# An encoder layer on one core: two heads' value products in turns, last rows picked with plain 0/1 matrices in fp32r halves, one turn moved

## The chip, the core and the metric

The kernel runs on 1 core of one Trainium2 chip. The metric is the device time of one execution in microseconds, the median of the runs. Engines: TensorE (PE in the profile; PEld is its weight load), VectorE (DVE), ScalarE (ACT), GpSimd (POOL), SyncE (SP, which here only issues DMAs).

## What is computed

One layer of a streaming encoder over 544 tokens (512 of a new stream, 32 of a running one) of width 1024, all in float32:

```python
h = rmsnorm(x, g_norm_mix)
cq, ckv, kpe, gq, gk, gv, glr, gr, ga, gb = split_cols(h @ w_in)
o_a = mla_attention(...)          # 8 heads, 64-wide values, chunk-causal
o_g, s_new = gla(...)             # 4 heads, matrix state 128 x 256, decaying
o_b = rmsnorm(o_g, g_gla_norm) * silu(gr)
merged = sigmoid(ga) * (o_a @ w_branch_a) + sigmoid(gb) * (o_b @ w_branch_b)
x = x + merged @ w_out
y = hier_moe(rmsnorm(x, g_norm_ffn), ...)   # 32 experts, the best 2 of one group of 8 per token
x = rmsnorm(x + y, g_norm_final)
```

An expert is `(silu(xb @ w_gate) * (xb @ w_up)) @ w_down` with 1024 x 512 weights: 6 MB per expert, 32 experts. A token's two expert rows are added with two gates.

## The kernel before

**Products in three parts.** The large projections run as fp32r matmuls. A weight tile `raw` is split in a high half `whi` (ScalarE, `high`) and a low half `wlo` (GpSimd, `split`, L909), the activations likewise, and `product` (L1055) adds high x high, high x low and low x high: 48 matmuls of 272 columns for eight blocks of K. The order of products is a list written out by hand (`weight_tiles`, `outputs`). Results go to two PSUM slots `proj` in turn; the next product but one waits until ScalarE or VectorE has read its slot (`proj_read`).

**Attention.** 40 units `u` = (head pair, row block, head of the pair). Row blocks 0 to 3 have 128 queries and 1 to 4 blocks of keys, block 4 (the running stream) has 32 queries and three blocks. The loop L1216 is a software pipeline on TensorE: `scores(u)`, a third of a filling projection (`product_part`, 16 matmuls, until the list is used up), `turn_probs(u - 2)` (transposes into bank 2), `pv(u - 3)` (value product into bank 3, head `a` in partitions 64a to 64a + 63). VectorE takes the maximum and normalises, ScalarE exponentiates (`exps`) and copies the turned probabilities out (`copy_turned`, which may not overwrite `probT[u % 2]` before the value product of unit u - 2). `copy_out` on VectorE splits the pair's output after both heads. All of these are fp32 matmuls, each of which is two records in the trace.

**GLA and branches.** After the recurrent part, VectorE normalises outputs (`normed_output`, L2368; L2383 for the running stream), ScalarE copies the high half (`o_high`, 0 to 4), and the low half `ob_lo` is made by GpSimd for the first `EARLY_LOW` parts (`low_output`, L917, placed in GpSimd's queue behind the split of `wa` 5 and ahead of that of `gb` 0) and by VectorE for the rest (L2390). TensorE meanwhile runs `ga` 5 and `wa` 5, then `gb` 0 and `wb` 0. `gb` 0 needs the slot of `ga` 5, read by the sigmoid of `gate_value(0, "ga", 5)` (L1907), and its own split weights; `wb` 0 needs the slot of `wa` 5, read by VectorE's `branch(0, 5)`, and all five parts of `ob_lo`.

**Routing.** VectorE finds each token's experts, slots and gates. `on_lanes` (L1498) multiplies one-hot matrices (`lanes`, slot of the block; values by block of 64 slots) to give each lane its token: twenty fp32 records each, two halves of 64 lanes in turns. `unread` and the loop L1491 are idle products. Two times five transposes (L1528) then spread the gates of the tokens for experts 30 and 31 along the free dimension. GpSimd gathers the token rows by these numbers; `turn_rows` (L1564) turns them.

**Experts.** Weights flow in three sets of buffers (`load_expert`, L817) as sets come free. Per expert `up` (L1538, L1540: two halves of the array in turns), Silu on ScalarE, the product on VectorE (L2541), `turn_hidden` (L1547), `down` (L1554, L1555). Rows of experts 0 to 29 are scattered to DRAM and read back (`zc`, L890) once all are stored. The load of `zc` stands in the queue behind the weights.

**The end.** Experts 30 and 31 skip the way through DRAM. Their rows stay in `yo`, and `last_rows` (L1631) multiplies `pick[s]`, a matrix of slot by token holding the gate where they meet, with `yo` in two row halves of 64 slots, into PSUM; for row blocks 1 to 3 `second_rows` (L1642) adds the gated second rows. VectorE adds the first rows with their gates (`add_gated`, L2617), then PSUM (`add_last`, L2624), ScalarE sums the squares (L1717) and takes the root (L1719), VectorE applies `final` (L2635). Expert 30's turn stands between the up products of 30 and 31.

## Time and profile before

| | us |
|---|---|
| median of 3 runs (lowest to highest) | 1121.83 (1120.65 to 1122.44) |
| the profiled execution | 1119.33 |
| its span, first to last instruction | 1117.5 |
| TensorE busy | 1028.3 (92%) |
| VectorE, ScalarE, GpSimd busy | 384.0, 282.0, 221.3 |
| attention's value products (first to last start) | 105.5 to 250.3 |
| first products of the `gb`, `wb` branch | 421.4 |
| expert weights: first request | 562.5 |
| first down rows of expert 30 turned | 1077.1 |
| mean DMA rate over the span | 239 GB/s |

A matmul's busy time is modelled to its end, so records that follow each other overlap: the distance between two starts tells what a group costs the engine, and where groups are merged in a timeline row, the start of the next row ends it. In brackets stands the idle time ahead of a row and what ended it. An arrow points from what is read to what is written.

### The profile page before, as it was taken

The numbers are of one execution on the slowest core, as the hardware profiler recorded it, in microseconds if no ns is written. First come the engines' busy times: TensorE is split into PE (matmuls) and PEld (weight loads), VectorE is DVE, ScalarE is ACT, GpSimd is POOL, SyncE is SP. The second block draws the span as 40 slices with busy tenths as digits, with TensorE's granted clock in tenths as the row PEclk, the third lists the DMA queues.
The fourth block names the chain that finished last, engine by engine and source line by source line (L and its number), as shares of the span: only waits on it lengthen the run. The fifth ranks groups of instructions, "written<-read, shape, count | busy, mean of one in ns | idle before, by whom it ended". The sixth has DMA issues, their size and how long they took to land.

```text
span 1117.5 us, 15305 instructions
## 1 busy us (share of the span) xinstructions
PE 1028.3 (92%) x6339; PEld 701.7 (63%) x6339; DVE 384.0 (34%) x729; ACT 282.0 (25%) x455; POOL 221.3 (20%) x127
## 2 busy tenths in 40 slices
PE   8999999999999999999999899988888888778886
PEld 6996777869998879999998333333333333333232
DVE  7246232233587492421344322111111111111017
ACT  5435434346456542222213100000000000000003
POOL 0331122112322363434330011100111110110000
PEclk9999999999999989999999999988888998988898
DMA  8343411212212113253285999999999999999994
GB/s 224 89 91 88 159 39 40 56 38 76 58 48 56 50 57 94 78 165 103 78 352 225 345 427 428 425 427 425 427 427 427 427 428 428 426 429 426 426 412 156
DMA packets 108943, 267.57 MB, mean 239 GB/s; under 512 B 21821, under 2 KB 88797, under 8 KB 95666
## 3 DMA queue, kind: packets, MB, share of 16 engines
q1 hardware_dynamic: 104178, 258.06, 60.1%
q0 software_dynamic: 4704, 8.64, 2.0%
q8 instruction: 46, 0.75, 0.3%
q14 instruction: 15, 0.12, 0.0%
HBM read 256.12 MB, written 18.17 MB: 245 GB/s over the span
## 4 chain that ended last, share of the span: by engine, by line
PE 39%; DMA 23%; DVE 4%; issue 2%; ACT 2%; SPq 0%; DVEq 0%; ACTq 0%
DMA we<-in_w_exp_up 23%; PE proj L1055 17%; PE proj L1538 12%; PE proj L1554 3%; PE bank L1380 1%; PE bank L1430 1%; DVE xsT L2549 1%; PE proj L1336 1%; PE bank L1564 1%; ACT ex L1878 0%; PE proj L1540 0%; PE bank L1031 0%; PE bank L1631 0%; PE bank L1517 0%; SPq L817 0%
## 5 line engine op out<-in xcount | busy, mean ns | idle before, releaser
L1538 PE MATMUL proj<-we,xsT 128*64 128x512 f32 x512 | 255.7, 658 | 61.4 <-DMA we<-in_w_exp_up 51.8
L1540 PE MATMUL proj<-we,xsT 128*64 128x512 f32 x512 | 256.1, 658 | 0.0
L909 POOL TENSOR_TENSOR wlo<-raw,whi 128x1024 fp32r<-128x1024 f32 x68 | 155.8, 2292 | 396.7 <-PE proj L1055 369.1
L1538 PEld LDWEIGHTS proj<-we,xsT 128*64 128x64 f32 x512 | 74.3, 151 | 210.1 <-issue 197.1
L1055 PE MATMUL proj<-hT_hi,whi 128*128 128x272 f32 x688 | 146.6, 295 | 3.8 <-ACT sg L1907 3.8
L1055 PE MATMUL proj<-hT_hi,wlo 128*128 128x272 f32 x688 | 144.6, 292 | 0.0
L1055 PE MATMUL proj<-hT_lo,whi 128*128 128x272 f32 x688 | 144.5, 292 | 0.0
L2541 DVE TENSOR_TENSOR hg<-hg,proj 64x512 f32<-64x512 f32 x32 | 22.1, 690 | 308.8 <-ACT hg L2050 294.0
L2050 ACT ACTIVATE hg<-proj 64x512 f32<-64x512 f32 x30 | 17.8, 592 | 422.0 <-PE proj L1540 422.0
L1554 PE MATMUL proj<-we,hT 128*64 128x512 f32 x256 | 115.2, 592 | 1.1 <-DVE hT L2544 1.1
L1555 PE MATMUL proj<-we,hT 128*64 128x512 f32 x256 | 115.2, 592 | 0.0
L1055 PEld LDWEIGHTS proj<-hT_hi,whi 128*128 128x128 f32 x688 | 109.1, 190 | 6.6 <-ACT sg L1907 4.0
L1055 PEld LDWEIGHTS proj<-hT_lo,whi 128*128 128x128 f32 x688 | 109.0, 191 | 1.6 <-issue 0.9
L1055 PEld LDWEIGHTS proj<-hT_hi,wlo 128*128 128x128 f32 x688 | 108.6, 191 | 1.6 <-issue 0.9
L947 POOL DMA_INDIRECT expert_out<-yo,sidx x30 | 29.9, 997 | 386.7 <-DVE sidx L2561 386.7
L1696 ACT CAST whi<-raw 128x1024 fp32r<-128x1024 f32 x70 | 69.6, 997 | 109.7 <-PE proj L1055 102.1
L1554 PEld LDWEIGHTS proj<-we,hT 128*64 128x64 f32 x256 | 34.9, 137 | 71.3 <-issue 69.3
L1540 PEld LDWEIGHTS proj<-we,xsT 128*64 128x64 f32 x512 | 74.2, 151 | 0.0
L2558 DVE COPY yo<-proj 128x512 f32<-128x512 f32 x30 | 20.8, 692 | 66.1 <-PE proj L1555 66.1
L2211 DVE TENSOR_REDUCE stat<-bank 128x1 f32<-128x128 f32 (+4 forms) x40 | 19.2, 482 | 58.9 <-PE bank L1182 50.3
L1555 PEld LDWEIGHTS proj<-we,hT 128*64 128x64 f32 x256 | 34.9, 137 | 0.0
L1794 ACT ACTIVATE prob<-bank,stat 128x128 f32<-128x128 f32 (+4 forms) x40 | 20.9, 522 | 42.5 <-DVE stat L2211 42.2
(366 smaller groups left out, 1436.6 us busy)
## 6 DMA issues: line engine op xcount, KB each, us to landing
we<-in_w_exp_gate SPq DMA_DIRECT2D x31, 2048.0 KB, 32.2
we<-in_w_exp_up SPq DMA_DIRECT2D x31, 2048.0 KB, 36.8
we<-in_w_exp_down SPq DMA_DIRECT2D x31, 2048.0 KB, 38.8
raw<-in_w_in SPq DMA_DIRECT2D x43, 512.0 KB, 3.8
x_rows<-in_x_prompt SPq DMA_DIRECT2D x8, 512.0 KB, 4.8
raw<-in_w_branch_b SPq DMA_DIRECT2D x8, 512.0 KB, 4.1
raw<-in_w_out SPq DMA_DIRECT2D x8, 512.0 KB, 3.8
zc<-expert_out SPq DMA_DIRECT2D x4, 1024.0 KB, 17.3
```

The lines of the kernel that those rows point to most:

```text
L909: nc.gpsimd.tensor_tensor(lo[:, 0:c], raw[n % NRAW][:, 0:c], hi[:, 0:c].bitcast(F32), ALU.subtract).then_inc(w_split, 1)
L947: pool.indirect_dma_start(out=ys[:, :], out_offset=bass.IndirectOffsetOnAxis(ap=sidx[s][:, 0:1], axis=0), in_=yo[:, s, :], in_offset=None, ...
L1055: mm = pe.matmul(proj[:, slot, half, 0:HALF], w[:, at:at + P], r[:, k, half * HALF:(half + 1) * HALF], start=(m == 0), stop=(m == len(term ...
L1538: pe.matmul(proj[0:SLOTS, s, 0, :], xsT[:, k, cols], wg[:, k * FF:(k + 1) * FF], start=(k == 0), stop=(k == KD - 1))
L1540: mm = pe.matmul(proj[64:64 + SLOTS, s, 0, :], xsT[:, k, cols], wu[:, k * FF:(k + 1) * FF], start=(k == 0), stop=(k == KD - 1))
L1554: pe.matmul(proj[0:SLOTS, s, 1, :], hT2[:, s, k, :], wd[:, k * D:k * D + FF], start=(k == 0), stop=(k == 3))
L1555: mm = pe.matmul(proj[64:64 + SLOTS, s, 1, :], hT2[:, s, k, :], wd[:, k * D + FF:(k + 1) * D], start=(k == 0), stop=(k == 3))
L1696: nc.scalar.copy(whi[n % NHIGH][:, 0:c], raw[n % NRAW][:, 0:c]).then_inc(w_high, 1)
L1794: nc.scalar.activation(prob[u % 3][0:r, 0:n], bank[0:r, u % 2, 0:n], ACT.Exp, bias=stat[0:r, 1, u:u + 1], scale=-1.0, accum_out=stat[0:r, ...
L2211: v.tensor_reduce(stat[0:r, 1, u:u + 1], bank[0:r, u % 2, 0:n], AX.X, ALU.min).then_inc(negmax_ready, 1)
L2541: v.tensor_tensor(hg[0:SLOTS, s, :], hg[0:SLOTS, s, :], proj[64:64 + SLOTS, s, 0, :], ALU.mult).then_inc(done, 1)
L2558: v.tensor_copy(yo[:, s, :], proj[:, s, 1, :])
```

## The change

1. `pv` takes a pair of heads: for each block of keys the matmul of head 0 and that of head 1 follow each other. It is issued at u = 2v + 4, where so far the second head's stood; the first head's stood one step earlier.
2. `EARLY_LOW` is 2 instead of 3: part 2 of `ob_lo` goes from GpSimd to VectorE. On ScalarE `gate_value(0, "ga", 5)` comes before `o_high(3)` and `o_high(4)`.
3. The gates of experts 30 and 31 are brought to the lanes by two `on_lanes` products (2 columns) instead of ten transposes. They scale the rows of `yo`, and `pick[s]` is a plain 0/1 matrix. `yo` is held in fp32r as a high half (ScalarE) and a low half (VectorE, `low_rows`), and each pick has two fp32r matmuls for one in fp32; the pick for row block 0 waits for the low half.
4. The turn of expert 30's hidden rows moves from between the up products of 30 and 31 to the middle of those of 31.
5. ScalarE runs a one-column Sqrt behind the last Silu, and waits for `picks_ready` before the last rows.
6. A few buffers move: `xsb2` (used only if some expert has more than 64 rows) to behind `g_fin`, `yo_lo` to its place, and everything from the weight ring on by 64 bytes.

```diff
--- before.py
+++ after.py
@@ -121,7 +121,7 @@
-EARLY_LOW = 3
+EARLY_LOW = 2
@@ -340,7 +340,8 @@
     sidx = [R(f"sidx{n}", [P, 1], U32) for n in range(2)]
     gate = R("gate", [P, 2, NT])
-    last_gates = R("last_gates", [P, NT, 2])
+    last_gates = R("last_gates", [P, 2, NT, 2])
+    last_slots = R("last_slots", [P, 2])
     RING = R.at
...
@@ -527,6 +531,7 @@
     down_done = sem("down_done")
     yo_ready = sem("yo_ready")
+    low_y = sem("low_y")
     ys_zeroed = sem("ys_zeroed")
...
@@ -693,9 +697,12 @@
     U_ = Region(RT)
-    pick = [U_(f"pick{s}", [P, TOK]) for s in range(2)]
-    xsb2 = U_("xsb2", [P, D])
+    pick = [U_(f"pick{s}", [P, TOK], F32R) for s in range(2)]
+    yo_lo = U_("yo_lo", [P, 2, FF], F32R)
     assert U_.at <= LAST
+    xsb2 = nc.alloc_sbuf_tensor_at("xsb2", [P, D], F32, offset=G_FIN + D * 4)
+    assert G_FIN + 2 * D * 4 <= W_G2 + GH * DK * 4
     numbers = con("rope")
@@ -1195,24 +1202,26 @@
             mm.then_inc(probT_done, 1)
-        def pv(u):
-            hp, i, a = UNITS[u]
-            h = 2 * hp + a
+        def pv(v):
+            hp, i, _ = UNITS[2 * v]
             r = unit_shape(i)[0]
-            v = u // 2
-            pe.wait_ge(probT_copied, u + 1)
-            if a == 0 and v >= 1:
+            pe.wait_ge(probT_copied, 2 * v + 2)
+            if v >= 1:
                 pe.wait_ge(oa_done, v)
             blocks = key_blocks(i)
             for b, kr_, vb in blocks:
-                mm = pe.matmul(bank[64 * a:64 * a + 64, 3, 0:r],
-                               V[0:kr_, vb, h * VD:(h + 1) * VD], probT[u % 2][0:kr_, b * r:(b + 1) * r],
-                               start=(b == 0), stop=(b == len(blocks) - 1))
-            mm.then_inc(pv_done, 1)
+                for a in range(2):
+                    h = 2 * hp + a
+                    mm = pe.matmul(bank[64 * a:64 * a + 64, 3, 0:r],
+                                   V[0:kr_, vb, h * VD:(h + 1) * VD], probT[a][0:kr_, b * r:(b + 1) * r],
+                                   start=(b == 0), stop=(b == len(blocks) - 1))
+            mm.then_inc(pv_done, 2)
         keys(0)
         keys(1)
         NU = len(UNITS)
+        assert NU % 2 == 0 and all(a == u % 2 for u, (_, _, a) in enumerate(UNITS))
         for u in range(NU + 3):
@@ -1226,8 +1235,8 @@
             if 2 <= u < NU + 2:
                 turn_probs(u - 2)
-            if u >= 3:
-                pv(u - 3)
+            if u >= 4 and u % 2 == 0:
+                pv(u // 2 - 2)
@@ -1521,12 +1530,8 @@
         pe.wait_ge(last_gates_ready, 1)
-        for s in range(2):
-            row = proj[:, s, :, :].rearrange("p a b -> p (a b)")
-            for i in range(NT):
-                r = ROWS[i]
-                mm = pe.transpose(row[:, i * P:i * P + r], last_gates[0:r, i, s:s + 1].to_broadcast([r, P]), ident[0:r, 0:r])
-            mm.then_inc(gate_rows_done, 1)
+        on_lanes(proj[:, 0, 0, 0:2], 0, last_gates, True, False)
+        on_lanes(proj[:, 0, 0, 0:2], 1, last_gates, False, True).then_inc(gate_rows_done, 1)
@@ -1628,7 +1633,12 @@
             for half in range(2):
                 rows_ = slice(64 * half, 64 * half + 64)
-                mm = pe.matmul(out[0:r, half, :], pick[s][rows_, i * P:i * P + r], yo[rows_, s, :], start=start, stop=stop)
+                pe.matmul(out[0:r, half, :], pick[s][rows_, i * P:i * P + r], yo_hi[rows_, s, :], start=start, stop=False)
+            if i == 0:
+                pe.wait_ge(low_y, s + 1)
+            for half in range(2):
+                rows_ = slice(64 * half, 64 * half + 64)
+                mm = pe.matmul(out[0:r, half, :], pick[s][rows_, i * P:i * P + r], yo_lo[rows_, s, :], start=False, stop=stop)
             if stop:
@@ -1641,7 +1651,11 @@
                 pe.matmul(out[:, half, :], second[:, i - 1, :], zc[i][:, 1, half * FF:(half + 1) * FF], start=start, stop=False)
         def up_half(k):
+            if k:
+                pe.wait_ge(act_done[0], PAIRS)
+                turn_hidden(0, hT2_done)
             for part in range(2):
@@ -1657,8 +1671,6 @@
             pe.wait_ge(n0[part], loads)
         up(0, slice(0, SLOTS), w0[0], w0[1], up_done)
-        pe.wait_ge(act_done[0], PAIRS)
-        turn_hidden(0, hT2_done)
         up(1, slice(SLOTS, P), w1[0], w1[1], up_done, up_half)
@@ -1983,9 +1995,9 @@
         nc.scalar.activation(ors_d[:, :, :], bank[:, 1, 0:GH * DEC].rearrange("p (h l) -> p h l", l=DEC), ACT.Sqrt, bias=eps_col[:, :])\
             .then_inc(o_rms, 1)
+        gate_value(0, "ga", 5)
         o_high(3)
         o_high(GH)
-        gate_value(0, "ga", 5)
         out_of("wa", 5)
@@ -2065,13 +2077,16 @@
         act.wait_ge(up_done, NE)
         nc.scalar.activation(hg[0:SLOTS, 1, :], proj[0:SLOTS, 1, 0, :], ACT.Silu).then_inc(silu_done, 1)
+        nc.scalar.activation(st_x[:, 1, 0:1], eps_col[:, :], ACT.Sqrt)
         act.wait_ge(all_stored, 1)
+        act.wait_ge(picks_ready, 1)
         act.wait_ge(down_done, NE - 1)
-        nc.scalar.copy(yo[:, 0, :], proj[:, 0, 1, :]).then_inc(last_y, 1)
+        nc.scalar.mul(yo_hi[:, 0, :], proj[:, 0, 1, :], last_slots[:, 0:1]).then_inc(last_y, 1)
         act.wait_ge(hT2_done, NE)
         nc.scalar.copy(hT2[:, 1, :, :], bank[:, 3, 0:4 * SLOTS].rearrange("p (k l) -> p k l", k=4)).then_inc(hT2_copied[1], 1)
         act.wait_ge(down_done, NE)
-        nc.scalar.copy(yo[:, 1, :], proj[:, 1, 1, :]).then_inc(last_y, 1)
+        nc.scalar.mul(yo_hi[:, 1, :], proj[:, 1, 1, :], last_slots[:, 1:2]).then_inc(last_y, 1)
@@ -2516,8 +2531,8 @@
         run(v.reciprocal(gate[:, 0, :], r5[2]))
         run(v.tensor_tensor(gate[:, 1, :], gate[:, 0, :], rd, ALU.mult))
-        run(v.tensor_tensor(both_gates, O[:, :, :, NE - 2:NE], gate[:, :, :].unsqueeze(3).to_broadcast([P, 2, NT, 2]), ALU.mult))
-        v.tensor_tensor(last_gates[:, :, :], both_gates[:, 0], both_gates[:, 1], ALU.add).then_inc(last_gates_ready, 1)
+        v.tensor_tensor(last_gates[:, :, :, :], is_blk[:, :, :, NE - 2:NE], gate[:, :, :].unsqueeze(3).to_broadcast([P, 2, NT, 2]), ALU.mult)\
+            .then_inc(last_gates_ready, 1)
@@ -2530,10 +2545,10 @@
         dve.wait_ge(meta_ready, 1)
         dve.wait_ge(late_loaded, 32)
+        dve.wait_ge(gate_rows_done, 1)
+        v.tensor_copy(last_slots[:, :], proj[:, 0, 0, 0:2])
         for s in range(2):
-            dve.wait_ge(gate_rows_done, s + 1)
-            row_ = proj[:, s, :, :].rearrange("p a b -> p (a b)")[:, 0:TOK]
-            last = v.scalar_tensor_tensor(pick[s][:, :], numbers, G1[:, NE - 2 + s:NE - 1 + s], row_, ALU.is_equal, ALU.mult)
+            last = v.tensor_scalar(pick[s][:, :], numbers, G1[:, NE - 2 + s:NE - 1 + s], None, ALU.is_equal)
         last.then_inc(picks_ready, 1)
@@ -2611,6 +2626,11 @@
             gated(s, act_done[s])
+        def low_rows(s):
+            dve.wait_ge(last_y, s + 1)
+            v.scalar_tensor_tensor(yo_lo[:, s, :], proj[:, s, 1, :], last_slots[:, s:s + 1], yo_hi[:, s, :].bitcast(F32),
+                                   ALU.mult, ALU.subtract).then_inc(low_y, 1)
         def add_gated(i, c):
@@ -2635,9 +2655,11 @@
                 .then_inc(y_last, 1)
+        low_rows(0)
         add_gated(0, 0)
         step.settle()
         add_gated(0, 1)
+        low_rows(1)
         add_gated(1, 0)
```

## Rows read from the trace of the kernel before

**Rows 1.** the page's 40 slices: share of the DMA engines, in tenths

```profile
DMA  8343411212212113253285999999999999999994
```

**Rows 2.** busy time of each engine by stretch, with granted clock and DMA

```profile
core 0: us, PE busy (x) PEld busy (x) DVE busy (x) ACT busy (x) POOL busy (x), PEclk, DMA share, GB/s
200.00:220.00 20.00, 20.00 (x139) 16.18 (x137) 6.18 (x21) 8.00 (x20) 4.73 (x2) 1.00 0.12 29
...
422.30:425.60 3.30, 3.30 (x17) 3.30 (x17) 0.00 (x0) 0.91 (x1) 2.37 (x1) 0.51 0.00 0
426.00:430.00 4.00, 4.00 (x34) 4.00 (x33) 0.00 (x0) 0.77 (x2) 0.66 (x1) 1.00 0.46 131
633.00:1068.00 435.00, 372.85 (x1650) 145.41 (x1648) 76.02 (x176) 17.75 (x30) 43.55 (x43) 0.91 1.01 426
1102.40:1115.10 12.70, 5.71 (x22) 1.42 (x18) 12.26 (x14) 4.33 (x9) 0.00 (x0) 0.87 0.34 136
```

**Rows 3.** timeline, TensorE, attention: start, duration, line, out<-in, shapes, count

```profile
105.53 0.43 PE L1208 MATMUL bank<-probT,V 128*64 128x128 f32 x2
105.90 0.91 PE L1178 MATMUL bank<-kcat,qT 96*128 96x384 f32 x2
...
212.17 1.09 PE L1208 MATMUL bank<-probT,V 128*64 128x128 f32 x8
213.19 0.49 PE L1178 MATMUL bank<-kcat,qT 96*128 96x128 f32 x2
...
220.28 0.64 PE L1208 MATMUL bank<-probT,V 128*64 128x32 f32 x6
```

**Rows 4.** timeline of TensorE where tiles of 32 and 64 columns take turns

```profile
343.14 1.08 PE L1283 MATMUL bank<-ex 128*32 128x128 f32 x32
344.15 0.66 PE L1287 MATMUL bank<-cst,ex 128*128 128x128 f32 x4
...
616.73 0.92 PE L1498 MATMUL bank<-token_at,lanes 128*64 128x48 f32 x20 [0.25 <-DVE token_at L2493]
617.58 0.92 PE L1498 MATMUL bank<-is_blk,lanes 128*64 128x48 f32 x20
```

**Rows 5.** timeline of TensorE at the end of attention

```profile
249.31 1.19 PE L1208 MATMUL bank<-probT,V 128*64 128x32 f32 x12 [0.54 <-DVE oa_lo L2230]
```

**Rows 6.** timeline of all engines around the first branch products

```profile
401.50 1.42 DVE L2368 SCALAR_TENSOR_TENSOR gqk<-gqk,gains,ors 128x512 f32<-128x512 f32 x2
...
408.20 7.54 POOL L917 TENSOR_TENSOR ob_lo<-gqk,ob_hi 128x1024 fp32r<-128x1024 f32 x3
...
410.84 0.37 ACT L1984 ACTIVATE ors_d<-bank,eps_col 128x128 f32<-128x128 f32 x1
411.08 5.22 DVE L2368 SCALAR_TENSOR_TENSOR gqk<-gqk,gains,ors 128x512 f32<-128x512 f32 x2
...
415.71 2.83 POOL L909 TENSOR_TENSOR wlo<-raw,whi 128x1024 fp32r<-128x1024 f32 x1
...
419.41 1.28 ACT L1907 ACT_TABLE_LOAD   x1
...
421.38 0.52 PE L1055 MATMUL proj<-hT_hi,whi 128*128 128x272 f32 x2 [3.76 <-ACT sg L1907]
```

**Rows 7.** timeline of TensorE in the routing stage

```profile
620.25 1.52 PE L1528 MATMUL proj<-cst,last_gates 128*128 128x128 f32 x10
```

**Rows 8.** timeline of TensorE and VectorE behind the last weights

```profile
1077.12 0.69 PE L1547 MATMUL bank<-cst,hg 64*128 64x64 f32 x4 [1.41 <-DVE hg L2541]
...
1091.89 3.83 DVE L2617 SCALAR_TENSOR_TENSOR x_rows<-zc,gate,x_rows 128x1024 f32<-128x1024 f32 x3 [5.69 <-DMA zc<-expert_out]
...
1094.62 1.02 PE L1631 MATMUL bank<-yo,pick 64*128 64x512 f32 x4
...
1098.66 1.22 DVE L2624 TENSOR_TENSOR x_rows<-x_rows,proj 128x1024 f32<-128x1024 f32 x1 [0.32 <-PE proj L1631]
...
1102.49 1.22 DVE L2624 TENSOR_TENSOR x_rows<-x_rows,bank 128x1024 f32<-128x1024 f32 x1 [1.34 <-PE bank L1631]
```

More of the change, by code:

```diff
@@ L465, in _build @@
     hT2 = K_("hT2", [P, 2, 4, SLOTS])
+    YO = K_.at
     yo = K_("yo", [P, 2, FF])
+    yo_hi = nc.alloc_sbuf_tensor_at("yo_hi", [P, 2, FF], F32R, offset=YO)
     W_ = Region(K_.at)
@@ L685, in _build @@
     expert = T_("expert", [P, 2, NT])
-    both_gates = T_("both_gates", [P, 2, NT, 2])[:, :, :, :]
     extra = T_("extra", [P, NE])[:, :]
```

## The prediction

> **What bounds the kernel now.** I read the page's 40 slices first, for the regime of each part, then busy time by stage, and then the timeline engine by engine where the edits lie. Over the last 17 slices the DMA engines are full [rows 1]; from 633 to 1068 us they carry 426 GB/s with a share of 1.01, while TensorE is idle for 62 of 435 us [rows 2]. This is the stream of 32 experts' weights. A faster matmul inside it buys nothing: its length is bytes over rate. It starts when the branch products are done, so all that ends earlier ahead of it moves the whole stream, and the end with it. Ahead of it TensorE is the bound: in attention it is busy 20.00 of 20.00 us at clock 1.00 [rows 2]. Two stretches therefore matter: TensorE's path before the stream, and what follows the stream's last bytes.
>
> **Value products in turns.** Now each unit (one head, one row block) has its own value product in the left or right 64 columns of the array. It occupies TensorE for 105.90 − 105.53 = 0.37 us with one block of keys and 213.19 − 212.17 = 1.02 us with four [rows 3], so (1.02 − 0.37)/3 = 0.217 us per further block: 0.37, 0.58, 0.80, 1.02. The sample's block, with 32 columns moved, takes 0.58 (six records, of which the last drains beyond it; bounds 0.52 and 0.64 [rows 3]). One head: 3.35 us; eight: 26.8 us, all on the path.
> The change issues both heads' matmuls block by block in turns. What would two half-array matmuls side by side cost? The trace has such orders elsewhere. 32 records in 32-column tiles of the same 128 moved columns take 344.15 − 343.14 = 1.01 us, that is 0.126 us for four side by side [rows 4]. 20 records in 64-column tiles, alternating halves and moving 48 columns, take 617.58 − 616.73 = 0.85 us, 0.085 per pair [rows 4]. A single record now has 0.217/2 = 0.108. So a pair costs between 0.108 (nothing lost) and 0.126; I take 0.117, the middle, as nothing says which end. Over 4 head pairs × 20 records that is 0.7 us lost against perfect overlap. Pairing saves 13.4 − 0.7 = 12.7 us.
> "TensorE: Matmul & The Clock Gate" of the Trainium skill (section on LDWEIGHTS) speaks against the small block: a load costs its columns divided by 1.2, 53 ns for 64, so 107 ns for two heads' loads. By that rule six pairs of the sample block would cost 0.64 us and the four pairs together save 0.2 to 0.3 us less. The rows disagree: two 64-column loads and their matmuls fit in 85 ns [rows 4].
> What is late next: the copy of an even unit's turned probabilities must now wait for the value products of the pair before it, as these are issued one unit later. ScalarE queues behind that wait the next exponential and an eviction. TensorE wants the copy only after the next scores and 16 filling matmuls (about 2 us), and the copy follows the pair at once, so I charge nothing there. At the end of attention no filling is left. There the chain is value pair, copy of unit 38, turn of unit 39, copy, last pair, and the 0.54 us that TensorE already waits for VectorE [rows 5] stays. Adding the copies and turns as they follow each other, I charge 0.9 us, with bounds 0.3 and 1.6. **Attention: −11.8 us, bounds −10.5 and −13.**
>
> **Order on ScalarE and EARLY_LOW 2.** TensorE stands still for 3.76 us until 421.38, on the sigmoid of `ga` 5 [rows 6]. ScalarE is free from 411.2, but makes two copies `o_high` first, which wait for VectorE. It turns to the sigmoid only at 419.41 (table load 1.28, then 0.62) [rows 6]. Put ahead of them, it needs just the product of `ga` 5, which ends 24 matmuls of 4.0/34 = 0.118 us [rows 2] before the standstill at 417.6, so at about 414.8; the sigmoid is out by 415.4 to 416.7. The next bar is the weight split of `gb` 0 on GpSimd, ending at 415.71 + 2.83 = 418.5 behind three `low_output` (7.54 us) [rows 6]. With two of them (5.03) GpSimd is free at 413.2, starts after the product at 414.8, and ends by 417.6 at the latest. Neither is later than 417.6: the standstill goes.
> Third bar: the `wb` 0 product, 48 matmuls (5.7 us) later at 423.3, needs all parts of `ob_lo` and VectorE's `branch(0, 5)`. VectorE's two `L2368` last 5.22 us beside GpSimd's work against 1.42 without it [rows 6]; with one GpSimd operation less they end some 1.5 us earlier. VectorE gains the moved subtraction: bounds 1.2 us (half of GpSimd's 2.51) and 1.2 + 2.4 if it is held again. I add up to VectorE done at 422.3, or 424 when held at each step; I take no wait, bound 0.7.
> Here the rule bears against the edit: "GPSIMD Engine Reference" of the Trainium skill (Specifications) says that GpSimd's SBUF interfaces are shared with VectorE, with contention for operations with two SBUF inputs. A subtraction moved to VectorE is such an operation. The 5.22 against 1.42 us agree.
> After the standstill the granted clock is 0.51 for 3.3 us: 17 records, where 34 take 4.0 at full clock [rows 2]. Its loss, 3.3 − 17 × 4.0/34 = 1.3 us, goes with the standstill. **Branch stage: −3.8 − 1.3 = −5.1, bounds −3 and −5.4.**
>
> **Gates on lanes.** Ten transposes (1.52 us with the drain, 1.35 of pitch) [rows 7] become two `on_lanes` of 0.85 each [rows 4]: +0.35 us ahead of the first turn of gathered rows. Weights already requested keep the DMA engines busy meanwhile, so part is hidden: **+0.2, bounds 0 and +0.4.** The picks on VectorE become cheaper but were hidden behind the gather. One small operation goes; nobody waits for it.
>
> **Behind the stream.** The turn of expert 30's hidden rows (0.69 us after 1.41 of waiting) [rows 8] moves inside the next up products. But VectorE's tail starts when the stored rows land at 1091.89 [rows 8], behind the weights in the queue. The turn buys slack and no time: 0. Picks: two fp32 records per half become two fp32r ones. Four side by side take 0.9 to 1.0 us now [rows 8]; by the products' pace (0.118 us for 272 columns) the high and low records of 512 columns take 2 × 0.22 = 0.44. TensorE gains 0.45 at each of ten picks. VectorE pays two low halves; the second (0.7 us, PSUM and SBUF into 512 columns) lies on its path. VectorE waited 0.32 us for picks before 1098.66 and 1.34 before 1102.49 [rows 8]; from then on it is busy 12.26 of 12.70 us [rows 2, 8]. So the end comes earlier by 1.34 + 0.32 − 0.7 = 1.0 us at most, by −0.3 if a wait is left. The load of the Sqrt table (a table load takes 1.28 us [rows 6]) goes under the last products; in the tail it lies beside VectorE's combinations, which are busy without a wait for it, and is worth 0. **Tail: −1.0, bounds −1.3 and +0.7.**
>
> **Sum.** −11.8 − 5.1 + 0.2 − 1.0 = −17.7 us. The profiled execution took 1119.3 us (span 1117.5), so it would be 1101.6. The median of the runs shown, 1121.8, lies 2.5 above the profiled one, so I forecast 1104.1.
>
> **Rivals.**
> A. Two heads' products do not run side by side, their records being short and fp32 in two passes. Then 12.7 comes back: 1116.8. Against it stand both groups of rows 4, for it only that neither has exactly this form. 0.07.
> B. The branch stage keeps a wait in a new place: VectorE, held by GpSimd as in the 5.22 us, delivers `ob_lo` and `branch(0, 5)` 2 us or more after 423.3, and the slow clock follows again (1.3). That gives 1107.4 to 1109. 0.10.
> C. Row halves in fp32r don't overlap: a pick costs 4 × 0.22 = 0.88, as now, and the low halves come on top: tail +0.7, 1105.8. 0.10, within the main range.
> D. Slower than before: attention falls to the half clock. The pace of rows 2 makes each us of full-clock work 1.65 us; the gain of 17.7 is gone once 27 us of attention's work run so, and at 35 us the time is 1127. Against it: clock 1.00 with TensorE full, and the odd units lose matmuls but no filling. 0.03.
> The forecast has 0.70.
>
> **Range and chances.** The parts' bounds, taken together with one unit of run spread (1120.65 to 1122.44), give 1100 to 1108 for the forecast alone. B reaches to 1109, so 1099.5 to 1109.5 leaves out A, D and about 0.06 of larger surprises. A measurement of this kernel tells about 0.2% (2.2 us) from no change. Faster by more: 0.96; within: 0.01; slower: 0.03.
>
> **What would show it.** In the changed profile: value products of a four-block pair within 1.0 to 1.15 us, none in odd units, attention over 11 to 12 us earlier; no standstill before `gb` 0 and no slow clock behind it; first expert weights requested some 17 us earlier; 426 GB/s as before; VectorE without idle time between the first combination and the last row. It is wrong if value records follow one another at 0.108 us, if the standstill has moved to `wb` 0, or if the stream's length changes.

## The result, and the profile after

The changed kernel takes 1102.76 us (median of 4 executions, 1101.24 to 1103.72) beside 1121.24 us for the kernel before: 18.5 us less, ratio 0.9833 with a 95% interval of 0.9816 to 0.9851. The forecast was 17.7 us less. The profiled execution took 1103.72 us (span 1101.6), that of before 1119.33. In a second comparison the same kernel gained only 15.4 us (below, x9); what differs between the two turned out to be the main lesson. One of the nine executions of the kernel before in the last series below took 2498.14 us; it counts in the median given there, but not in the intervals.

| us, profiled executions | before | after | difference |
|---|---|---|---|
| first scores of attention | 96.08 | 97.01 | +0.93 |
| from there to the first gate product behind attention | 154.93 | 142.27 | −12.66 |
| from there to the last 512-column means | 143.11 | 143.06 | −0.05 |
| last 512-column means to the first of the small means | 12.53 | 12.52 | −0.01 |
| from there to `wb` 0 (the branch stage) | 22.38 | 16.82 | −5.56 |
| `wb` 0 to the first expert's up product | 196.90 | 197.35 | +0.45 |
| first up product to the first stored rows added | 465.96 | 467.99 | +2.03 |
| from there to the end of the last `final` (the tail) | 23.18 | 22.19 | −0.99 |

Attention of after, timeline of TensorE (start, duration, line, out<-in, shapes, count, and in brackets the idle time ahead and what ended it). It answers to [rows 3] and [rows 5]:

```profile
206.45 1.09 PE L1216 MATMUL bank<-probT,V 128*64 128x128 f32 x16
207.47 0.49 PE L1185 MATMUL bank<-kcat,qT 96*128 96x128 f32 x2
...
235.57 0.31 PE L1202 MATMUL bank<-cst,prob 32*128 32x32 f32 x3 [0.85 <-DVE prob L2234]
235.81 1.09 PE L1216 MATMUL bank<-probT,V 128*64 128x128 f32 x16
237.43 0.31 PE L1202 MATMUL bank<-cst,prob 32*128 32x32 f32 x3 [0.53 <-ACT probT L1819]
238.10 0.66 PE L1216 MATMUL bank<-probT,V 128*64 128x32 f32 x12 [0.37 <-ACT probT L1819]
239.28 1.38 PE L1247 MATMUL bank<-w_g,glr 96*128 96x512 f32 x4 [0.52 <-DVE oa_lo L2245]
```

Sixteen records of two heads take 207.47 − 206.45 = 1.02 us. In [rows 3] eight records of one head took exactly that. The last rows show what came in place of the filling work: waits at the end of attention.

The branch stage of after, timeline of ScalarE, GpSimd and VectorE, and one stretch of busy time with granted clock. They answer to [rows 6] and to the half-clock row in [rows 2]:

```profile
402.86 0.63 ACT L1919 ACTIVATE sg<-proj 128x544 f32<-128x544 f32 x1 [2.30 <-PE proj L1062]
```

```profile
396.41 4.76 POOL L924 TENSOR_TENSOR ob_lo<-gqk,ob_hi 128x1024 fp32r<-128x1024 f32 x2
402.97 2.41 POOL L916 TENSOR_TENSOR wlo<-raw,whi 128x1024 fp32r<-128x1024 f32 x1 [1.81 <-PE proj L1062]
```

```profile
399.29 3.09 DVE L2383 SCALAR_TENSOR_TENSOR gqk<-gqk,gains,ors 128x512 f32<-128x512 f32 x2
...
405.72 4.89 DVE L2405 TENSOR_TENSOR ob_lo<-gqk,ob_hi 128x1024 fp32r<-128x1024 f32 x3
410.53 0.71 DVE L2352 TENSOR_TENSOR msum<-proj,sg 128x544 f32<-128x544 f32 x1
```

```profile
core 0: us, PE busy (x) PEld busy (x) DVE busy (x) ACT busy (x) POOL busy (x), PEclk, DMA share, GB/s
404.00:411.70 7.70, 7.70 (x64) 7.70 (x63) 7.25 (x6) 2.73 (x4) 4.60 (x2) 1.00 0.41 111
```

TensorE is busy in every microsecond up to `wb` 0, at clock 1.00. GpSimd's split for `gb` 0 ends at 402.97 + 2.41 = 405.38, and `gb` 0 starts at 405.67: 0.29 us are left there. VectorE's `branch(0, 5)` ends at 411.24, and `wb` 0 starts at 411.68: 0.44 us are left before the third bar bites.

The tail of after, timeline of VectorE, against [rows 8]:

```profile
1077.02 2.61 DVE L2637 SCALAR_TENSOR_TENSOR x_rows<-zc,gate,x_rows 128x1024 f32<-128x1024 f32 x2 [2.62 <-DMA zc<-expert_out]
1079.55 0.74 DVE L2631 SCALAR_TENSOR_TENSOR yo_lo<-proj,last_slots,yo_hi 128x512 fp32r<-128x512 f32 x1
...
1084.11 1.22 DVE L2644 TENSOR_TENSOR x_rows<-x_rows,proj 128x1024 f32<-128x1024 f32 x1
...
1086.63 1.22 DVE L2644 TENSOR_TENSOR x_rows<-x_rows,bank 128x1024 f32<-128x1024 f32 x1
```

The two waits for picks (0.32 and 1.34 us) are gone and the low half (0.74) has come: 23.18 − 22.19 = 0.99 us saved.

Two rows of the table have no term in the prediction. Attention's first scores start between 96.08 us (before) and 99.26 us (x2) in the 14 profiles of this document, in kernels whose code ahead of them is the same, so the 0.93 us say nothing of the change. And the second expert ran partly at the half clock in this execution; from its first up product to its first down product it takes 8.61 us, against 6.92 before, which is 1.69 of the 2.03 us:

```profile
core 0: us, PE busy (x), PEclk, DMA share, GB/s
616.00:623.00 7.00, 5.50 (x22) 0.76 1.00 383
```

Whether the change has a part in that is open: it is seen in three of the nine profiles whose kernels have the new gates and picks (after, x4, x11), and in none of the five without.

### The profile page after: what moved, and what is told of

Same layout as the page of the kernel before. It is cut to its first block, busy times and chain, and to the rows that moved or that the text cites. A ratio compares the mean times of both kernels' runs of the same rounds, so it can differ in the third digit from the quotient of the medians.

```text
span 1101.6 us, 15368 instructions
## 1 busy us (share of the span) xinstructions
PE 1004.5 (91%) x6369; PEld 696.1 (63%) x6369; DVE 390.0 (35%) x732; ACT 281.0 (26%) x456; POOL 218.9 (20%) x126
## 4 chain that ended last, share of the span: by engine, by line
PE 38%; DMA 26%; DVE 4%; issue 2%; ACT 1%; SPq 0%; DVEq 0%; POOLq 0%; ACTq 0%
DMA we<-in_w_exp_up 24%; PE proj L1062 18%; PE proj L1543 11%; PE proj L1559 3%; DMA zc<-expert_out 1%; PE bank L1389 1%; PE bank L1439 1%; DMA expert_out<-yo,sidx 1%; PE bank L1569 1%; PE proj L1345 1%; DVE x_rows L2637 1%; DVE xsT L2564 1%; ACT ex L1890 1%; PE proj L1545 0%; DVE x_rows L2644 0%
## 5 line engine op out<-in xcount | busy, mean ns | idle before, releaser
L1543 PE MATMUL proj<-we,xsT 128*64 128x512 f32 x512 | 249.1, 644 | 69.6 <-DMA we<-in_w_exp_up 61.5
L1545 PE MATMUL proj<-we,xsT 128*64 128x512 f32 x512 | 249.5, 644 | 0.0
L2062 ACT ACTIVATE hg<-proj 64x512 f32<-64x512 f32 x30 | 17.7, 590 | 424.0 <-PE proj L1545 424.0
L1185 PE MATMUL bank<-kcat,qT 96*128 96x128 f32 (+4 forms) x80 | 30.0, 456 | 0.4 <-ACT kcat L1793 0.4
```

The costliest lines, as they stand in the source:

```text
L1185: mm = pe.matmul(bank[0:r, u % 2, 0:n], qT[0:QK, h, q0:q0 + r], kcat[hp % 2][0:QK, a, k0:k0 + n], start=True, stop=(i == 4))
L1543: pe.matmul(proj[0:SLOTS, s, 0, :], xsT[:, k, cols], wg[:, k * FF:(k + 1) * FF], start=(k == 0), stop=(k == KD - 1))
L1545: mm = pe.matmul(proj[64:64 + SLOTS, s, 0, :], xsT[:, k, cols], wu[:, k * FF:(k + 1) * FF], start=(k == 0), stop=(k == KD - 1))
```

## The experiments

Three series of executions of the kernel before stand beside them: 1119.45 us for x1 to x4, 1120.03 us for x5 to x7 and x9, 1120.89 us for x8 and x10 to x12. All differences from here on are against these. x5 to x7 and x9 ran on another chip than the other experiments. What is read from a trace comes from one execution of each kernel. Rows of busy time without a head line have the columns of the second expert's row above (stretch, its length, TensorE's busy time with its records, granted clock, DMA share, GB/s).

### Does each part carry its own term? (x1, x2, x3)

x1_pairs_only puts only the paired value products into the kernel before:

```diff
...
-            if u >= 3:
-                pv(u - 3)
+            if u >= 4 and u % 2 == 0:
+                pv(u // 2 - 2)
```

> The kernel before with the paired value products alone. Theory (two heads' products run side by side at the price of one): attention 12.7 us shorter, so 1121.2 - 12.7 = 1108.5 us, a four-block pair in 1.02 us, and the standstill before the gb branch still there. Rival 1 (most of the gain is the later, single place of the pair, with fewer interruptions, and not the overlap): the time is the same here too, so this kernel does not tell it apart; x4_pair_in_sequence does. Rival 2 (the gain of attention is partly given back in the branch stage, where VectorE and GpSimd were hidden by it): over 1110 us.

Measured: 1108.72 us, 10.7 less (ratio 0.99, 0.9883 to 0.9917). In its trace attention takes 142.35 us, 12.58 less than before, and the standstill ahead of `gb` 0 is still there with 3.73 us. Attention's term is confirmed in the trace; the time shows 2 us less of it. Most of that is given back in the tail, which is 24.93 us long here, 1.75 more than before. VectorE's rows of x1, to be read against [rows 8]:

```profile
1080.18 2.61 DVE L2617 SCALAR_TENSOR_TENSOR x_rows<-zc,gate,x_rows 128x1024 f32<-128x1024 f32 x2 [3.96 <-DMA zc<-expert_out]
...
1085.72 1.22 DVE L2624 TENSOR_TENSOR x_rows<-x_rows,bank 128x1024 f32<-128x1024 f32 x1 [1.49 <-PE bank L1631]
...
1088.70 1.22 DVE L2624 TENSOR_TENSOR x_rows<-x_rows,proj 128x1024 f32<-128x1024 f32 x1 [0.56 <-PE proj L1631]
...
1092.53 1.22 DVE L2624 TENSOR_TENSOR x_rows<-x_rows,bank 128x1024 f32<-128x1024 f32 x1 [1.34 <-PE bank L1631]
```

It now waits three times for picks. The stored rows landed at 1080.18, but the first pick behind the last expert's products starts only at 1083.69, 3.51 us later (before, 1091.89 and 1093.65: 1.76 us). From that pick to the end it is 21.42 us in both. So in these two kernels the end hangs on TensorE's last products and not on the stored rows. Why those products came later here is open.

x2_branch_only:

```diff
-EARLY_LOW = 3
+EARLY_LOW = 2
...
+        gate_value(0, "ga", 5)
         o_high(3)
         o_high(GH)
-        gate_value(0, "ga", 5)
```

> The kernel before with ScalarE's gate of ga 5 ahead of the two high copies and with EARLY_LOW 2, nothing else. Theory: standstill of 3.8 us and the slow clock behind it (1.3 to 1.7 us) both go, 1121.2 - 5.5 = 1115.7 us, wb 0 starts without a wait. Rival (the wait moves to wb 0, on VectorE's branch(0, 5) or its low parts): about 2 us less gain, 1117.5 to 1119 us.

Measured: 1114.52 us, 4.9 less (0.9961, 0.9943 to 0.9979). No idle time ahead of `gb` 0 or `wb` 0; from the small means to `wb` 0 it takes 16.82 us against 22.38, as in the changed kernel.

x3_rest_only leaves out both and keeps gates, picks, turn and Sqrt:

```diff
+            if k:
+                pe.wait_ge(act_done[0], PAIRS)
+                turn_hidden(0, hT2_done)
...
-        for s in range(2):
-            row = proj[:, s, :, :].rearrange("p a b -> p (a b)")
...
+        on_lanes(proj[:, 0, 0, 0:2], 0, last_gates, True, False)
+        on_lanes(proj[:, 0, 0, 0:2], 1, last_gates, False, True).then_inc(gate_rows_done, 1)
```

> The kernel before with only the parts behind the branch stage: gates on lanes, plain picks in two halves, the moved turn, the early Sqrt. Theory: tail -1.0, routing +0.2, so 1121.2 - 0.8 = 1120.4 us, hardly to be told from no change in the time; in the trace the stretch from VectorE's first combination of stored rows to the last final operation is 22.2 us against 23.2. Rival (the low halves on VectorE's path cost what the picks save): 23.2 us or more, 1121.4 us or more.

Measured: 1119.6 us, no difference that can be told (0.9999, 0.9988 to 1.001; 1115.41 to 1121.62 in ten executions). In the trace the tail is 1088.99 to 1111.18, 22.19 us, against 23.18: the 1.0 us is there. But the trace also shows where it is spent: from `wb` 0 to the first expert's up product it takes 197.93 us against 196.90, 1.03 us more. In the five profiles without the new gates and picks that distance is 196.88 to 196.94 us, in the nine with them 197.35 to 198.52.

### Overlap, or only one place? (x4)

```diff
-            for b, kr_, vb in blocks:
-                for a in range(2):
+            for a in range(2):
+                for b, kr_, vb in blocks:
```

> The changed kernel with the matmuls of a pair in another order: all blocks of one head, then all of the other, at the same place in the queue, same work. Theory (the gain is the overlap of the two halves of the array while they take turns): a four-block pair takes 2.04 us instead of 1.02 and the kernel 1102.8 + 13.4 = 1116.2 us. Rival (the gain comes from issuing the pair at one place): within 2 us of 1102.8.

Measured: 1107.7 us, 11.75 less than before (0.9902, 0.9884 to 0.992). Both expectations missed: the order costs about 5 us (1107.7 against 1102.76, and 5.36 in the trace of attention), not 13.4 and not nothing. Its timeline of TensorE:

```profile
110.41 0.44 PE L1216 MATMUL bank<-probT,V 128*64 128x128 f32 x4
110.78 0.91 PE L1185 MATMUL bank<-kcat,qT 96*128 96x384 f32 x2
...
117.75 0.66 PE L1216 MATMUL bank<-probT,V 128*64 128x128 f32 x8
118.34 1.13 PE L1185 MATMUL bank<-kcat,qT 96*128 96x512 f32 x2
...
134.34 1.58 PE L1216 MATMUL bank<-probT,V 128*64 128x128 f32 x16
135.85 0.49 PE L1185 MATMUL bank<-kcat,qT 96*128 96x128 f32 x2
...
142.00 1.22 PE L1216 MATMUL bank<-probT,V 128*64 128x32 f32 x12
143.15 0.70 PE L1185 MATMUL bank<-kcat,qT 96*128 96x256 f32 x2
```

| us from one start to the next | two heads apart (before, twice the single of [rows 3]) | in sequence (x4) | in turns (after) |
|---|---|---|---|
| 1 block | 0.74 | 0.37 | 0.37 |
| 2 blocks | 1.16 | 0.59 | 0.59 |
| 3 blocks | 1.60 | 1.07 | 0.81 |
| 4 blocks | 2.04 | 1.51 | 1.02 |
| sample, 32 columns moved | 1.16 | 1.15 | 0.59 |
| sum | 6.70 | 4.69 | 3.38 |

Over four head pairs, standing next to each other saves 4 × 2.01 = 8.0 us and taking turns another 4 × 1.31 = 5.2; the stage of x4 is 147.63 − 142.27 = 5.36 us longer than that of the changed kernel. So two heads in sequence overlap too, but only in part. With 128 columns moved, up to four records of the second head run beside the last of the first. A single record takes 0.108 us, and 0.15 us of each distance belong to no record (0.37 − 2 × 0.108). By that 8 + 8 records take (1.51 − 0.15)/0.108 = 12.6 steps, 6 + 6 take 8.5, 4 + 4 take 4. With 32 columns nothing overlaps in sequence (1.15 = 2 × 0.58). Why, stays open.

### Which bar holds the branch stage? (x5, x6)

x5_order_only has the order of x2 with EARLY_LOW 3; x6_low_only has EARLY_LOW 2 with the old order.

> The kernel before with ScalarE's order alone changed; EARLY_LOW stays 3. Theory (two bars stand one behind the other): the sigmoid is no longer late, but GpSimd's split for gb 0 is, behind three low parts: it ends near 418.5 in the times of before, 0.9 us behind the last product of wa 5. The standstill shrinks from 3.8 to 0.9 to 1.3 us, so 2.5 to 2.9 us are gained, 4.2 if the slow clock behind it goes too; 1115 to 1117 us. Rival (ScalarE's order is all that counts): the standstill is gone and the gain is 5.5 us, as with both edits.

Measured: 1117.4 us, 2.6 less (0.9977, 0.9967 to 0.9988). Timeline of TensorE and GpSimd of x5, and busy time behind the standstill:

```profile
419.06 0.49 PE L1055 MATMUL proj<-hT_hi,whi 128*128 128x272 f32 x2 [1.82 <-POOL wlo L909]
```

```profile
408.55 7.59 POOL L917 TENSOR_TENSOR ob_lo<-gqk,ob_hi 128x1024 fp32r<-128x1024 f32 x3
416.10 5.19 POOL L909 TENSOR_TENSOR wlo<-raw,whi 128x1024 fp32r<-128x1024 f32 x2
```

```profile
419.06:423.50 4.44, 4.44 (x23) 0.62 0.62 168
```

The releaser has changed from ScalarE's `sg` to GpSimd's `wlo`, as the second bar demands, but 1.82 us remain, not 0.9 to 1.3, and the half clock stays.

> The kernel before with EARLY_LOW 2 alone; ScalarE keeps its order. Theory: the sigmoid still stands behind the two copies, but VectorE is held by GpSimd for a shorter time, so that its parts come about 1.3 us earlier and the standstill is 2.5 us instead of 3.8; 1.3 us gained, 1118 us. Rival (the low part on GpSimd is what delays the product): gain of 3.8 us or more.

Measured: 1118.23 us, 1.8 less (0.9983, 0.9973 to 0.9993). The standstill is 2.37 us and still ends with the sigmoid. So each edit alone leaves a wait on the other's bar, and only both together remove it. The profile of x6 has a second wait, though, one of 1.99 us ahead of `ga` 5 (below), which the profile of before lacks. Its 2.37 us are therefore not simply 3.76 less what the edit saves.

### Does the moved turn buy anything? (x7)

```diff
-            if k:
-                pe.wait_ge(act_done[0], PAIRS)
-                turn_hidden(0, hT2_done)
...
+        pe.wait_ge(act_done[0], PAIRS)
+        turn_hidden(0, hT2_done)
         up(1, slice(SLOTS, P), w1[0], w1[1], up_done, up_half)
```

> The changed kernel with expert 30's turn back between the up products of experts 30 and 31. Theory (the turn buys slack, no time): the same time as the changed kernel on this chip within 0.5 us, and VectorE's tail begins when the stored rows land, in both. Rival (the turn brings expert 30's rows early enough to matter): 0.7 us or more slower, with VectorE waiting in the tail.

Measured: 1102.59 us (1099.84 to 1106.45), not to be told from x9. In the trace VectorE's tail begins with the stored rows in both, but here it waits 0.26 us for expert 31's high half at `low_rows(1)`, and the tail is 22.53 us against 22.22 in x9. That is not shown to be the turn's work: x8, x10 and x12 below have the moved turn, and the same wait (0.20 to 0.22 us) and the same tail (22.47 to 22.50 us). VectorE's row of x10:

```profile
1078.07 0.75 DVE L2634 SCALAR_TENSOR_TENSOR yo_lo<-proj,last_slots,yo_hi 128x512 fp32r<-128x512 f32 x1 [0.22 <-ACT yo_hi L2092]
```

In these four profiles the stored rows landed 465.5 to 465.7 us behind the first up product, in the others of kernels with the new picks 466.1 us or more. From the first up product to the end x7 takes 488.19 us and the other three 487.97 to 488.13. The turn buys no time that can be told.

### The changed kernel once more (x9)

> The changed kernel as it is, on the chip of these comparisons and in more rounds. If the parts measured alone (10.7, 4.9 and about 0 us) add up, it is 15.6 us faster than before; by its trace it should be 17 to 19 us, since the tail's 1.0 us and the routing's 0.2 us are too small for the spread, and half-clock stretches come and go by up to 3 us. I expect 17.5 us.

Measured: 1104.63 us (1099.84 to 1104.73), 15.4 less than before (0.9852, 0.9836 to 0.9869). The sum of the parts (15.6) is met, the 17.5 us expected are not. Its profile has a wait that the first profile of the same kernel did not have. Timeline of TensorE and busy time of x9:

```profile
396.07 0.82 PE L1062 MATMUL proj<-hT_hi,whi 128*128 128x272 f32 x2 [1.98 <-DVEq L2335]
```

```profile
core 0: us, PE busy (x), PEclk, DMA share, GB/s
239.00:244.00 5.00, 5.00 (x20) 0.50 0.00 0
396.07:401.80 5.73, 5.73 (x25) 0.50 0.83 235
```

Now the profiles of all kernels can be set side by side in the two stretches ahead of `wb` 0: from the last 512-column means (L1380, L1389) to the small means, and from there to `wb` 0. In brackets stands which of the two branch edits a kernel has:

| us | first stretch | second stretch | sum |
|---|---|---|---|
| before, x1 (neither edit) | 12.5 | 22.4 | 34.9 |
| after (both) | 12.5 | 16.8 | 29.3 |
| x5 (order alone) | 11.0 | 20.4 | 31.4 |
| x2, x4, x7 (both) | 11.0 | 16.8 | 27.8 |
| x6 (EARLY_LOW alone) | 9.3 | 23.2 | 32.5 |
| x3 (neither edit) | 9.3 | 21.5 | 30.8 |
| x9, x8 (both) | 9.3 | 21.6 | 30.9 |
| x10, x12 (both, and the fill ahead of `ga` 5, below) | 9.3 | 19.0 | 28.3 |
| x11 (both, and the fill behind attention, below) | 10.8 | 17.4 | 28.3 |

The first stretch is the same work everywhere. Its busy time in after, x4 and x9, in this order:

```profile
core 0: us, PE busy (x), PEclk, DMA share, GB/s
382.34:394.86 12.52, 12.52 (x50) 0.73 0.00 1
386.85:397.84 10.99, 10.99 (x50) 0.84 0.00 1
382.93:392.23 9.30, 9.30 (x51) 1.00 0.01 2
```

It takes 12.5 us where the granted clock is 0.73 in it, 11.0 at 0.84 and 9.3 at 1.00. Where it is quickest, TensorE comes to `ga` 5 before VectorE has released the slot: the S update is held behind L2383 (L2368 in the kernel before). VectorE's row of x9, beside GpSimd's weight splits:

```profile
390.32 3.98 DVE L2383 SCALAR_TENSOR_TENSOR gqk<-gqk,gains,ors 128x512 f32<-128x512 f32 x2
```

TensorE waits 1.98 us, and in x3, x8 and x9 then runs at clock 0.50 or 0.51 for at least 5.5 us. There the branch edits gain nothing: 30.8 without (x3, which has no standstill at `gb` 0), 30.9 with them. Where the first stretch is slowest they gain the full 5.6.

But the wait doesn't bring the half clock by itself. x6 has the same quick first stretch and the same wait, and its clock stays. Timeline of TensorE and busy time of x6:

```profile
409.44 0.52 PE L1055 MATMUL proj<-hT_hi,whi 128*128 128x272 f32 x2 [1.99 <-DVEq L2320]
```

```profile
409.44:415.00 5.56, 5.56 (x44) 1.00 0.80 232
```

There the standstill at `gb` 0 is back with 2.37 us, and the sum is 32.5, more than in x3 with neither edit.

How much of the two gains, 18.5 and 15.4 us, does this explain? 1.2 of the 3.1 us between them are the medians of the kernel before (1121.24 and 1120.03). The profile of x9 is 1.6 us longer than that of after in these two stretches and 1.4 us longer between attention and them (144.43 against 143.06), and after lost 1.7 us in the second expert. Such stretches are large enough for the rest, but the other executions have no trace, and the chips of the two comparisons may differ. So it is likely and not shown that the rest comes from such stretches.

### Fills in the waits (x8, x10, x11, x12)

x10 puts one idle product of 0.96 us ahead of `ga` 5:

```diff
+        pe.wait_ge(o_rms, 3)
+        for _ in range(1):
+            pe.matmul(bank[:, 3, :], ident, cst[:, 0:512], start=True, stop=True)
         product("ga", 5)
```

> The changed kernel with one idle product (0.96 us) ahead of ga 5, where TensorE waited 1.98 us for VectorE in some executions and then ran 8 us at clock 0.63. Theory (the wait sets off that slow stretch, and an engine half as idle keeps its clock): in such executions ga 5 to wb 0 takes 15.1 us instead of 17.8, so 2.7 us less; in the others the idle product costs up to 1 us. Four of the five executions on this chip looked like the first kind, so the median goes from 1104.6 to 1102.5 us. Rival (the clock falls all the same): 1104.6 to 1105.6 us, with clock 0.63 behind a wait of 1.0 us.

Measured: 1101.98 us, 18.9 less (0.9829, 0.9815 to 0.9844), and its five executions lie within 1.0 us (1101.39 to 1102.36) where those of x9 lay within 4.9. Timeline of TensorE and busy time:

```profile
393.88 1.11 PE L1420 MATMUL bank<-cst 128*128 128x512 f32 x2
396.02 0.52 PE L1062 MATMUL proj<-hT_hi,whi 128*128 128x272 f32 x2 [1.03 <-DVEq L2338]
```

```profile
239.00:244.00 5.00, 5.00 (x21) 0.50 0.00 0
396.02:401.70 5.68, 5.68 (x45) 1.00 0.77 225
```

The product starts at the same distance as in x9, but at clock 1.00: 18.99 us to `wb` 0 in place of 21.62. x12 below has the same fill, a wait of 1.04 us and clock 1.00 too. With the full wait three of four profiles ran at the half clock, with half of it filled none of two. That the fill is what kept the clock is likely, as the small spread of x10 says too, and not shown: x6 kept it with the full wait.

x11 puts idle products of 128 or 256 columns into the waits at the end of attention:

```diff
+            if u >= NU:
+                pe.wait_ge(exp_done, min(u - 1, NU))
+                n = (256, 128, 128)[u - NU]
+                pe.matmul(bank[:, 0, 0:n], ident, cst[:, 0:n], start=True, stop=True)
             if 2 <= u < NU + 2:
                 turn_probs(u - 2)
...
+        pe.matmul(bank[:, 0, 0:256], ident, cst[:, 0:256], start=True, stop=True)
         pe.wait_ge(oa_done, 20)
```

> The changed kernel with idle products of 0.24 to 0.48 us in the four waits of 0.85, 0.53, 0.37 and 0.52 us that now end attention. Theory (these waits set off the half clock of 240.3 to 243.4 us behind it, which costs 1.5 us): clock 1.00 there and 1 to 1.5 us less. Rival (they lie on the chain of copies and turns, and the clock falls as it did before the change): no gain, up to 0.3 us more.

Measured: 1101.87 us, 19.0 less (0.9822, 0.9798 to 0.9845). Attention has not become longer (142.30 us), and behind it:

```profile
239.00:244.00 5.00, 5.00 (x33) 1.00 0.00 0
```

From the first gate product to the last 512-column means it takes 141.52 us, against 143.06 (after) and 144.43 (x9). But x4 has no fill, has such waits at the end of attention, and also takes 141.52 us. Its first row behind attention, and its busy time there:

```profile
245.33 1.19 PE L1247 MATMUL bank<-w_g,glr 96*128 96x512 f32 x4 [0.51 <-DVE oa_lo L2245]
```

```profile
244.00:249.00 5.00, 4.49 (x35) 1.00 0.01 3
```

x2 and x5, with attention as before, take 141.57. So this half clock too comes and goes by itself (absent in three of twelve profiles without the fill, and in both with it), and that the fill removed it is not shown. The fill does not help further on: the stretch with the 512-column means ran at 0.84 in this profile, with no wait directly ahead of it.

x8 puts two idle products into the wait behind the first expert's up products:

```diff
+                if first_pair(it, m) and s == 0:
+                    unread(2)
                 pe.wait_ge(consts_set, 1)
                 pe.wait_ge(act_done[s], it * NSETS + m + 1)
                 turn_hidden(s, hT2_done)
```

> The changed kernel with two idle products (1.9 us) in TensorE's wait of 1.5 us behind the first expert's up products. Theory (the half-clock stretch in the second expert, which cost 1.8 us in two of the profiles and was absent in others, is set off by that wait): it is never seen, and executions are at most 0.4 us longer where it was absent, 1.5 us shorter where it was there; median about 1103 to 1104 against 1104.6 of the same chip. Rival (it comes without regard to that wait): 1104.6 or more.

Measured: 1102.92 us (1100.07 to 1105.32), 18.0 less (0.983, 0.9804 to 0.9856). Not settled: the second expert ran at 1.00 with the fill in both profiles that have it (x8, x12), but also in nine of twelve without it; the distance from the first up product to the stored rows is 465.5 to 466.4 us in those and 467.6 to 468.1 in the other three (after, x4, x11).

x12 has all three fills.

> The changed kernel with all three fills. If each works, 1099.5 to 1101 us and a smaller spread than the 4.9 us between the changed kernel's executions on this chip; if the clock falls without regard to them, 1105 to 1106 us.

Measured: 1099.35 us (1099.06 to 1102.69), 21.5 less than before (0.9815, 0.9796 to 0.9835). The three stretches in its profile, all at clock 1.00:

```profile
239.00:244.00 5.00, 5.00 (x38) 1.00 0.00 0
393.32:399.00 5.68, 5.68 (x45) 1.00 0.78 227
614.00:621.00 7.00, 7.00 (x30) 1.00 1.01 409
```

It has the lowest median of all kernels here, 3.4 us under the changed kernel's first and 5.3 under its second. The intervals of the ratios overlap for the first (0.9816 to 0.9851) and not for the second (0.9836 to 0.9869), so that it beats the changed kernel is likely and not certain. Which of the fills does it is not shown.

## Why the prediction was right, point by point

- **Value products.** The pair was priced at 0.117 us a record, between bounds of 0.108 and 0.126. It is the lower bound: 16 records in the 1.02 us of 8, nothing lost at any size. The sample pair takes 0.59 us. By the Trainium skill ("TensorE: Matmul & The Clock Gate", section "LDWEIGHTS (loading the stationary operand)") its twelve loads alone would take 0.64 us, an estimate from columns divided by 1.2; the trace is below that, as [rows 4] already were. The pairing saves 4 × 3.32 = 13.3 us (6.70 − 3.38 = 3.32) where 12.7 were priced, so the term was 0.6 us too careful. The end of attention was charged with 0.9 and costs 13.3 − 12.66 = 0.6. Attention: −12.66 against −11.8, inside the bounds.
- **Branch stage.** −5.1 was forecast, −5.56 measured in the profiles (beyond the bound of −5.4), and the reasons hold: the sigmoid is out in time, GpSimd's split is next in line (x5), both edits are needed (x5, x6), and `wb` 0 finds its parts with 0.44 us to spare. The difference is in how records were counted. The 34 records in 4.00 us include some that reach into the stretch or out of it; from start to start they come every 0.125 us and not every 0.118. `gb` 0 takes 429.03 − 421.38 = 7.65 us before and 411.68 − 405.67 = 6.01 after, so the slow clock cost 1.64 and not 1.3. From the start that `gb` 0 would have had (417.46, 0.25 us behind the last pair of records of `wa` 5) to 421.38 it is 3.92 us. Together that is 5.56. Rival B was close, those 0.44 us being all the room there was. What was missed is that the term has no single value. It was read from one execution in which the means ahead ran at a low clock. It is 5.6 us there, and nothing where they run at full clock and `ga` 5 then falls to the half clock (x3 against x9); as a median of executions it is 4.9 (x2). "It goes with the standstill" holds for the half clock behind `gb` 0, but in x9 and x8 a half clock stands two products earlier, behind the wait of 1.98 us.
- **VectorE beside GpSimd.** Two L2383 take 3.09 us with two low parts on GpSimd, 5.22 with three and 1.42 with none [rows 6], 3.98 beside GpSimd's weight splits (x9). The gain of a removed GpSimd operation there was taken as 1.5 us and was 5.22 − 3.09 = 2.1.
- **Gates on lanes.** This term was too small. The two `on_lanes` take 604.79 − 603.25 = 1.54 us, not 1.70; the transposes took 1.44 by the same measure (from 620.25 in [rows 7] to the next row at 621.69), not 1.35. So the products cost 0.1 us more. But the whole distance from `wb` 0 to the first up product grows by 0.45 us in after, and by 0.45 to 1.6 in the nine profiles with parts 3 to 6 of the change, where +0.2 was forecast with a bound of +0.4. In after 0.35 of the 0.45 us lie ahead of the gate products (191.57 us from `wb` 0 to them, against 191.22), and what makes them is open.
- **Tail.** −0.99 against −1.0. The fp32r halves overlap (rival C falls): a row pair in 0.23 us, where the estimate was 0.22. The turn was priced at nothing, and nothing can be told from it (x7). But the tail was measured from the landing of the stored rows, and the end doesn't hang on that alone: in x1 the tail grew by 1.75 us with the old picks, as TensorE's last products came later.
- **Rivals.** A falls with x4's table, D with attention's busy TensorE; the half clock did come behind attention, but for 3 to 6 us and in the kernel before too.
- **Signs.** The four-block pair takes 1.02 us, there is no wait at `gb` 0 or `wb` 0, the first expert weights are requested 17.25 us earlier (545.28 against 562.53), and the DMA engines carry 426 GB/s from 633 to 1060 us in both. One sign of being wrong did appear: from the first up product to the stored rows it takes 2.03 us longer, most of it the second expert's half clock. So by after, x4 and x11 the stream's length is not bytes over rate alone: a delay of TensorE at its start was not made up behind it.
- **The sum.** The terms give −18.8 in the trace (−12.66 − 5.56 + 0.45 − 0.99). The profiled execution shows −15.9 in span, since it began attention 0.9 us later and lost 2.0 in the second expert. The median fits the forecast of 1104.1 to 1.3 us in one comparison and to 0.5 in the other; part of that closeness is luck, as the gain moves by 3 us between the comparisons, and as attention and branches gained 1.3 us more than forecast, while the gates and the second expert lost 2.3.

## What to carry to other kernels

Put matmuls for different column groups next to each other and let them take turns block by block: next to each other alone gave about 60% of the gain here, the turns the rest. Before a stall is priced, read the same stretch in several executions: a fix behind a stretch whose clock varies was worth 5.6 us or nothing here. Read a tail from every engine that can end it: the tail with the old picks took 1.75 us more once the products ahead came later. After removing filling work, look for the short waits that it leaves behind, and try idle products there that end before the awaited data comes; with all three fills the median was the lowest here.

## What the runs showed of the hardware that was not expected

- Two 64-column groups fed one after the other, not in turns, overlap by about four records of 128 columns and by none of 32.
- A wait of 1.98 us was followed by 5.7 us at clock 0.50 (x9; likewise x3 and x8), but one of 1.99 us at the same place by 5.6 us at 1.00 (x6). One of 1.82 us (x5) was followed by 4.4 us at 0.62, while 1.03 us behind an idle product (x10) left it at 1.00. What decides between them is open.
- The clock also falls with no wait directly ahead: in the stretch with the 512-column fp32 means TensorE was busy throughout at 0.73 (after), 0.84 (x4) and 1.00 (x9), by the execution. What decides that is open.
- Arriving earlier can cost time: x8 and x9, 1.7 us quicker in that stretch than x4, were 3.1 us later at `wb` 0, counted from its start.
